# The start of the expert stage of a transformer layer: another order for the first experts' gathers, products and low parts

## What is computed

```python
scores = sigmoid(hf @ w_router)              # 512 x 16
# best group of 4 experts, in it the best 2, weights w_sel
for e in range(16):
    he = silu(hf @ w_gate[e]) * (hf @ w_up[e])        # 1024 -> 512
    y = y + combine[:, e:e + 1] * (he @ w_down[e])    # 512 -> 1024
```

## Time and profile before

| | |
|---|---|
| three timed runs | 768.83, 769.23 and 771.93 us |
| profiled execution, first to last instruction | 769.4 us |
| TensorE at work | 738.5 us, 96% of the span |
| VectorE | 587.7 us, 76% |
| ScalarE | 429.6 us, 56% |
| GpSimd | 95.5 us, 12% |
| moved by DMA | 172.72 MB, mean 224 GB/s |
| mean granted TensorE clock | 0.991 |

### The profile page before, as it was taken

One profiled execution on the slowest core, in us unless ns is written; L12 is line 12 of the kernel. 1 busy time (PEld: TensorE's weight loads), 2 busy tenths in 40 slices (PEclk: granted clock), 3 DMA queues, 4 the chain that ended last, 5 costly groups with the idle time before them and its releaser, 6 DMA issues. The chain is left out here.

```text
span 769.4 us, 10991 instructions
## 1 busy us (share of the span) xinstructions
PE 738.5 (96%) x4051; PEld 601.2 (78%) x4051; DVE 587.7 (76%) x817; ACT 429.6 (56%) x514; POOL 95.5 (12%) x131
## 2 busy tenths in 40 slices
PE   6899999999999999999999989999999999999994
PEld 5777999987877776878888757888888888888872
DVE  6967999797763545434666789888998999899988
ACT  5643344255445454652230246787788778887855
POOL 4010000000110000000000246311121111212002
PEclk9999999999999999999999999999999999999998
DMA  8547313420273111151349949999999999999163
GB/s 282 169 132 257 109 56 110 165 70 1 94 294 110 55 55 56 57 217 55 110 122 388 333 143 363 406 392 402 393 401 391 403 394 393 389 404 385 44 243 137
DMA packets 98547, 172.72 MB, mean 224 GB/s; under 512 B 15264, under 2 KB 35056, under 8 KB 98188
## 3 DMA queue, kind: packets, MB, share of 16 engines
q1 hardware_dynamic: 91200, 153.10, 55.2%
q0 software_dynamic: 4896, 12.95, 4.3%
q10 hardware_dynamic: 2412, 6.15, 2.1%
HBM read 161.83 MB, written 21.10 MB: 238 GB/s over the span
## 5 line engine op out<-in xcount | busy, mean ns | idle before, releaser
L2044 DVE TENSOR_TENSOR m_lo<-m_raw,m_hi 128x2048 fp32r<-128x2048 f32 x95 | 214.9, 2289 | 26.0 <-ACT m_hi L1008 22.9
L1008 ACT ACTIVATE m_hi<-m_raw 128x2048 fp32r<-128x2048 f32 x95 | 179.1, 1917 | 22.9 <-PE low L1156 22.4
L1154 PE MATMUL low<-m_hi,xe_hi 128*128 128x512 f32 x256 | 102.7, 401 | 0.7 <-DVE xe_lo L2180 0.5
L1156 PE MATMUL low<-m_hi,xe_lo 128*128 128x512 f32 x256 | 100.0, 391 | 0.0
L1155 PE MATMUL low<-m_lo,xe_hi 128*128 128x512 f32 x256 | 99.8, 390 | 0.0
L1154 PE MATMUL low<-hT_hi,w_hi 128*128 128x512 f32 (+1 forms) x240 | 94.5, 394 | 3.1 <-ACT smallT L767 1.2
L1155 PE MATMUL low<-hT_lo,w_hi 128*128 128x512 f32 (+1 forms) x240 | 92.0, 383 | 0.0
L1156 PE MATMUL low<-hT_hi,w_lo 128*128 128x512 f32 (+1 forms) x240 | 91.6, 382 | 0.0
L1731 DVE TENSOR_TENSOR w_lo<-raw,w_hi 128x2048 fp32r<-128x2048 f32 x27 | 61.8, 2290 | 37.2 <-ACT w_hi L737 37.0
L737 ACT ACTIVATE w_hi<-raw 128x2048 fp32r<-128x2048 f32 x28 | 53.5, 1909 | 16.5 <-PE wide L1156 8.3
L1154 PEld LDWEIGHTS low<-m_hi,xe_hi 128*128 128x128 f32 x256 | 48.1, 188 | 14.1 <-DVE m_lo L2044 3.7
(11 more groups left out here) (424 smaller groups left out, 1419.7 us busy)
## 6 DMA issues: line engine op xcount, KB each, us to landing
m_raw<-in_w_gate SPq DMA_DIRECT2D x32, 1024.0 KB, 8.0
m_raw<-in_w_up SPq DMA_DIRECT2D x32, 1024.0 KB, 7.9
m_raw<-in_w_down SPq DMA_DIRECT2D x31, 1024.0 KB, 8.3
raw<-in_w_in SPq DMA_DIRECT2D x19, 1024.0 KB, 5.7
raw<-in_w_out SPq DMA_DIRECT2D x4, 1024.0 KB, 5.1
y<-y_dram SPq DMA_DIRECT2D x8, 512.0 KB, 6.5
table_dram<-table_row ACTq DMA_DIRECT2D x1, 2624.0 KB
strips<-table_dram SPq DMA_DIRECT2D x8, 264.0 KB, 4.1
```

The lines of the kernel that those rows point to most:

```text
L1008: nc.scalar.activation(m_hi[n % MS][:, :], (m_spare if is_last(n, j) else m_raw[slot])[:, :], ACT.Copy).then_inc(q["m_hi_ready"], 1)
L1154: nc.tensor.matmul(outp, lh, rh, start=first, stop=False)
L1156: return nc.tensor.matmul(outp, ll, rh, start=False, stop=last)
L2044: v.tensor_tensor(m_lo[n % MS][:, :], (m_spare if is_last(n, j) else m_raw[n % MR])[:, :], m_hi[n % MS][:, :].bitcast(F32), ALU.subtract). ...
```

## The change

On POOL gather 1 waits until gather 0 has landed. On TensorE unit 0 of expert 0 is written out: first the products with the high rows, as soon as half of them is there, then those with the low rows; expert 1's rows are turned ahead of unit 3 rather than of unit 2; the list products of experts 2 and 3 stand behind unit 3 rather than ahead of it. On VectorE the low part of unit 0 stands ahead of the slots of expert 1, the low part of unit 1 behind the largest list length (`most`), then both halves of `xe_lo` and the low parts of units 2 and 3, and only then the remaining list steps up to `dest_ready` and the slots of experts 2 and 3. The part from `router_done` 5 on is as before.

```diff
@@ -655,6 +655,7 @@
 
             early_gather(0)
             pool.wait_ge(q["lists_ready"], 2)
+            pool.wait_ge(gathered[0], 16)
             early_gather(1)
             pool.wait_ge(q["dest_ready"], 1)
             for k in range(2 * TT):
@@ -1609,17 +1610,27 @@
             for _ in range(4):
                 nc.tensor.matmul(bank[4][:, :], m_hi[0][:, 0:P], m_hi[0][:, 0:512], start=True, stop=True)
             for u in range(4):
-                if u == 2:
-                    pe.wait_ge(q["xe_lo_ready"], 1)
+                if u == 3:
                     tokens(1, 16)
-                if u == 3:
-                    for t in range(2, TABLES):
-                        pe.wait_ge(q["chosen_ready"], t + 2)
-                        for i in range(TT):
-                            mm = nc.tensor.matmul(bank[2][:, 2 * t:2 * t + 2], slots[t][:, i, :], facts[:, i, t, :], start=(i == 0), stop=(i == TT - 1))
-                    mm.then_inc(q["router_done"], 1)
-                pe.wait_ge(q["xe_lo_ready" if u else "xe_half_lo"], 1)
+                if u == 0:
+                    pe.wait_ge(q["m_lo_ready"], 1)
+                    pe.wait_ge(q["xe_half_hi"], 1)
+                    wh, wl = (t[0][:, :].rearrange("p (c n) -> p c n", c=4) for t in (m_hi, m_lo))
+                    for k in range(4):
+                        nc.tensor.matmul(bank[0][:, :], xe_hi[:, k, :], wh[:, k, :], start=k == 0, stop=False)
+                        nc.tensor.matmul(bank[0][:, :], xe_hi[:, k, :], wl[:, k, :], start=False, stop=False)
+                    pe.wait_ge(q["xe_half_lo"], 1)
+                    for k in range(4):
+                        mm = nc.tensor.matmul(bank[0][:, :], xe_lo[:, k, :], wh[:, k, :], start=False, stop=False)
+                    mm.then_inc(q["m_used"], 1)
+                    continue
+                pe.wait_ge(q["xe_lo_ready"], 1)
                 m_unit(u + 1, u % MS, bank[u // 2][:, :], u % 2, xe_hi, xe_lo)
+            for t in range(2, TABLES):
+                pe.wait_ge(q["chosen_ready"], t + 2)
+                for i in range(TT):
+                    mm = nc.tensor.matmul(bank[2][:, 2 * t:2 * t + 2], slots[t][:, i, :], facts[:, i, t, :], start=(i == 0), stop=(i == TT - 1))
+            mm.then_inc(q["router_done"], 1)
             hidden(0)
 
             def expert_pe(j, s):
@@ -2157,12 +2168,20 @@
             slots_of(0, 1)
             dve.wait_ge(q["router_done"], 3)
             v.tensor_scalar(source_row[:, 0:1], bank[3][:, 0:1], -1.0, 0.0, ALU.add, ALU.max).then_inc(q["lists_ready"], 1)
+            m_split_lo(0)
             slots_of(1, 2)
             dve.wait_ge(q["router_done"], 4)
             lists_out(0, 2)
             step(v.tensor_copy(full(t1), ranks))
             step(v.tensor_reduce(gm[:, 0, :], bank[1][:, TT * NE:(TT + 1) * NE], AX.X, ALU.max))
             step(v.tensor_copy(most[:, :], gm[:, 0, :]))
+            m_split_lo(1)
+            for half, ready, done in ((0, "xe_half_hi", "xe_half_lo"), (1, "xe_hi_ready", "xe_lo_ready")):
+                dve.wait_ge(q[ready], 1)
+                v.tensor_tensor(xe_lo[:, 4 * half:4 * half + 4, :], bank[6 + half][:, :].rearrange("p (c x) -> p c x", c=4),
+                                xe_hi[:, 4 * half:4 * half + 4, :].bitcast(F32), ALU.subtract).then_inc(q[done], 1)
+            m_split_lo(2)
+            m_split_lo(3)
             step(v.scalar_tensor_tensor(out=full(t2), in0=full(t1), scalar=float(LISTS), in1=index16, op0=ALU.mult, op1=ALU.add))
             step(v.tensor_copy(rank_i[:, :, :], full(t1)))
             step(v.tensor_scalar(rank_i[:, :, :], rank_i[:, :, :], P.bit_length() - 1, None, ALU.logical_shift_right))
@@ -2174,15 +2193,7 @@
                 if k == 0:
                     step(ins)
             ins.then_inc(q["dest_ready"], 1)
-            m_split_lo(0)
-            for half, ready, done in ((0, "xe_half_hi", "xe_half_lo"), (1, "xe_hi_ready", "xe_lo_ready")):
-                dve.wait_ge(q[ready], 1)
-                v.tensor_tensor(xe_lo[:, 4 * half:4 * half + 4, :], bank[6 + half][:, :].rearrange("p (c x) -> p c x", c=4),
-                                xe_hi[:, 4 * half:4 * half + 4, :].bitcast(F32), ALU.subtract).then_inc(q[done], 1)
-            for n in range(1, 4):
-                m_split_lo(n)
-                if n == 2:
-                    slots_of(2, TABLES)
+            slots_of(2, TABLES)
             dve.wait_ge(q["router_done"], 5)
             lists_out(2, TABLES)
             m_split_lo(4)
```

## The result

Six runs of each kernel on one chip: the kernel after took 777.2 us (median; 776.6 to 779.6), the kernel before 770.6 us (768.8 to 773.4). The ratio is 1.0096, with a 95% interval of 1.0082 to 1.0111. The change makes the kernel slower, by 6.6 us by the medians and by 6.3 to 8.6 us by the interval; the sum that was forecast is 6.6 us. The 769.4 us that it starts from is a span, and in every run that lists both, the time is 1.7 to 2.5 us longer than the span. So the profiled execution of the kernel before took some 771 us or more, and that its span stood beside the median of three times (769.2; 770.6 with more runs) was chance.

What follows compares the result with a forecast made beforehand. The prediction took TensorE's pace in the expert loop as the bound; +2.2 + 0.6 - 0.7 - 0.2 + 3.1 + 1.6 = +6.6 us on 769.4 gave 776.0 us, range 771.0 to 780.5.

Steps and rivals of the forecast that it cites:

- Bound by TensorE: Expert loop: it runs at TensorE's pace, and at most 1.8 us of a delay ahead of it can be lost again.
- rival of earlier loads: Weight loads: buffer 0 is refilled up to 5.1 us sooner and the loop gains that, 764.3 us; chance 0.05.
- Low part ahead of the slots: Before the first turning: expert 1's slots come later, so TensorE's sixteen filler products begin 2.2 us later, +2.2.
- The fillers' clock: TensorE's filler products before the first turning: they run at the lower clock for 1.1 us more, +0.6.
- The first gather: Ahead of the first turning: taken to have landed by then, with the fillers setting the start; no term.
- High rows first: Unit 0 of expert 0: products without xe_lo cover its 0.7 us, so the unit starts that much earlier, -0.7.
- List products out of their place: Ahead of unit 3: the list products of lists 2 and 3 leave, about 0.2 us of loads not overlapped, -0.2.
- The second gather's wait: On Pool: held until the first gather lands, it is still there in time; worth nothing either way, 0.
- The chain behind unit 3: From unit 3's last product to hid's turning: list products and VectorE's steps take 4.88 instead of 1.82 us, +3.1.
- The clock again: Start of expert 1: after over 4 us of TensorE idle time, a stretch at 1.2 GHz, +1.6.
- rival of the clock that stays: Fillers and expert 1: the clock does not fall, so +2.7 in all, 772.1 us, or no change at 770.3; chance 0.13.
- Gather 2 just covered: Ahead of expert 2's turning: the gather lands at 490.2, TensorE wants it at 490.8, so it costs 0.

Runs made afterwards that it cites:

- e2: The kernel after with the low part of unit 0 put back behind the second list's slots, next to that of unit 1: 773.8 us, 1.0049 of before.
- e5: The kernel before with only the low part of unit 0 moved ahead of the slots of expert 1: 773.2 us against 770.7, ratio 1.0034.
- e9: The kernel before with only the second gather's wait until the first has landed: ratio 1.0001 to before.
- f1: The kernel after with gathers 2 and 3 issued ahead of all list writes on Pool: ratio 1.0107 to before.
- e3: The kernel after with 18 products into an unread bank added between the list products and the turning of hid: 777.0 us, 1.0081 of before.
- e4: The kernel after without the second gather's wait for the first: ratio 1.0113 to before.
- f3: The kernel after with the 18 added products behind the list products and gathers 2 and 3 ahead of the list writes: ratio 1.0071 to before.
- e6: The kernel before with only the high rows' products first in unit 0: ratio 0.9998 to before.
- e8: The kernel before with only the list products of experts 2 and 3 moved behind unit 3: 774.7 us, ratio 1.0057 to before.
- e1: The kernel after with VectorE's wait for the list products and lists_out(2, 4) moved behind hid: 781.5 us, ratio 1.0143 to before.
- f2: The kernel after with the list wait and lists_out(2, 4) behind hid, and gathers 2 and 3 ahead of the list writes: ratio 1.0069 to before.
- f4: The kernel after with low part 0 back, low part 3 behind the list steps, lists_out(2, 4) behind hid, gathers 2 and 3 first: 769.2 us against 770.2, 0.9986.

## Why the prediction was right

The direction, the size and the steps behind unit 3 held; ahead of them, what sets the turning of the first rows is another thing than was forecast. By its own steps, from the anchor:

- *Bound by TensorE.* Right: the loop's idle time is the same (1.79 us of 270, 1.82 of 280), and the 6.6 us that expert 2's rows are late (40.94 for 34.31) are nearly all still there at the end (6.8). The rival of earlier loads is refuted: the first load does move up to 451.32, and still the rows of experts 2 to 15 are all turned 6.6 to 7.1 us later than before.
- *Low part ahead of the slots, +2.2.* Measured 2.21 (fillers at 3.24 for 1.03). e2 and e5 show that it is this move. What that is worth at the turning comes next.
- *The fillers' clock, +0.6.* The fillers took longer by about that: from their start to the turning's, without its 0.27 us of idle time, 5.78 us pass (458.08 - 0.27 - 452.03) instead of 5.10, +0.68. But they do not set the turning in after; the first gather does. The prediction read from the order before that the fillers set it, and asked of the low parts only what they do to the list writes and gather 2, not to this gather, whose issue begins 1 us into it.
- *The first gather, no term of the sum.* There was little cover: in e9, with the order before, the gather lands 4.4 us after its issue, 0.65 us ahead of the turning. In after it lands 8.2 us after its issue, at 9.3 from the anchor. Five of the eight traces with the early low part turn the rows then, at 9.29 to 9.42. In f1 the fillers were done 1.16 us ahead, and the rows were turned at 9.31 all the same. In e3, e4 and f3, where the fillers end last, it is 9.45 to 9.65. So in after the rows are 3.16 us late because of the gather, and that the two terms' 2.8 us came near it is partly luck. Of the 3.8 us by which it lands later, 1.15 are its longer issue. The loads of 451.32 and behind, in flight beside it (DMA share 0.97 in 454 to 456), have a part too: the second gathers of e4 and e5, not held and beside such loads, landed after 6.8 and 6.6 us; those of before, e6 and e8 landed after 5.1 to 5.2, by 0.2 us at most past the first load's issue. The rest, about 1 us, stays open.
- *High rows first, -0.7.* Measured -0.83: unit 0 is 2.33 us late, the turning 3.16. Alone, in e6, it was worth nothing, since unit 1 then waited for its low part.
- *List products out of their place, -0.2.* From unit 0's start to the start of unit 3's last product 11.70 us pass (459.92 to 471.62) instead of 12.22: -0.5. The 0.3 beyond the forecast offset most of the missing 0.4 above; 0.24 of it is a stand ahead of unit 1 that the kernel before has and after has not.
- *The second gather's wait, 0.* Right in the order before (e9); e4 does not contradict it.
- *The chain behind unit 3, +3.1.* From unit 3's last product to hid's turning 4.89 us pass (4.88 forecast; 1.82 before): +3.07. e8 has the same wait alone, e1 and f2 halve it. Hid's turning is 4.88 us late in all; 5.0 was forecast.
- *The clock again, +1.6.* Measured 1.75 (13.22 us from hid to expert 2's rows instead of 11.47). It is not a fixed price: in the six traces where the clock falls there and no gather is waited for (after, e2, e4, e8, f1, f2) the stretch takes 12.84 to 13.92 us, 1.4 to 2.5 us more. The granted clock is 0.50 from 474 to 480; e3 and f3 keep it at 1.00 by work alone. The rival of the clock that stays is refuted.
- *Gather 2 just covered, 0.* Right, by the 0.6 us that were worked out: it was issued at 31.60 from the anchor (481.6 was forecast, which is 31.74) and landed 8.7 us later, at 489.1; its rows are turned from 489.73 without a wait. How thin that cover is, e1 and e3 show: each repairs one loss and meets the gather next.

So the sum held partly because two small errors cancelled. What the sum does not say is that its terms do not add when they are undone: e3 kept the clock up and had 0.2 us of it at expert 2's rows, and e1, which won 2.1 us of the chain, ended 3.1 us later, since a transfer stands 0.6 us behind.

## What to carry to other kernels

A product moved behind the unit that covered it brings along everything that another engine has queued behind its result: follow that engine's order to the next thing the bound engine needs, and add it up with its own durations. Before undoing a loss, ask what arrives next and by how much: here 0.6 us of cover decided that one right repair lost time and another gained none that is clear of noise, until the transfer was issued earlier. Ask the same of whatever an edit lets begin beside it: the first gather had 0.65 us of cover, and the low part moved beside its issue took that. An edit measured alone and the same edit in company can differ in worth (high rows first: 0 and 0.8 us), so try parts both ways.

## What was not expected of the hardware

The issue of an indirect DMA that Pool begins while a low part runs on VectorE, 0.02 us or more into it, ends 0.8 to 1.1 us past that low part's end, in the stretch of this change in all fourteen traces, however far that part has come: gather 0 of after ends at 452.22, the low part at 451.14; gather 2 at 483.24, its low part (480.09, 2.29 us) at 482.38; in e9 the second gather at 458.11, the low part (455.00, 2.28 us) at 457.28. One that began ahead of the low part was not held: f1's gather 2 began at 474.05, the low part at 474.35, and the issue took 0.93 us (above). So the time of a gather hangs on tenths of a microsecond.

The Trainium skill, SBUF — State Buffer, section "Who interferes with whom", infers that a tensor_tensor does not hold up GpSimd's descriptors, and says that one with two SBUF inputs contends with a GpSimd instruction that reads SBUF. The low part is such a one (m_raw and m_hi); the held issues, up to 3.10 us long, agree with the second sentence and not with the first.

The clock's fall is not settled by the code alone. e2 and f4 have the same work on TensorE and VectorE up to the first turning. Windows of e2 in the fillers:

```profile
449.00:450.00 1.00, 0.87 (x10) 0.78 (x11) 0.48 (x5) 0.00 (x0) 0.61 (x1) 0.77 0.00 0
450.00:451.00 1.00, 1.00 (x3) 0.75 (x3) 0.86 (x6) 0.00 (x0) 0.60 (x1) 0.50 0.00 0
```

The same of f4:

```profile
449.00:450.00 1.00, 0.87 (x11) 0.79 (x12) 0.48 (x5) 0.00 (x0) 0.61 (x1) 1.00 0.00 0
450.00:451.00 1.00, 1.00 (x6) 0.82 (x5) 0.86 (x6) 0.00 (x0) 0.59 (x1) 1.00 0.00 0
```

In f4 the clock stayed at 1.00 and TensorE then waited 1.03 us for the gather; in e2 it fell, and the fillers covered the gather. The rows were turned at 5.54 from the anchor in f4 and at 6.12 in e2.
